# Sample unit of a chunked state-space scan: state transposes, bank pairs and copies in another order

## The chip, the cores and the metric

One core of a Trainium2 chip runs the whole step. The metric is the device time of one execution in microseconds, the median of the runs. Engines are named as in the profile: PE is TensorE (matmuls and transposes), DVE is VectorE, ACT is ScalarE, POOL is GpSimd, SP is the queue that issues the DMAs (SPq in a row).

## What is computed

One step of a decoder layer for 512 prompt tokens and 64 sample tokens (8 sequences of 8). The change lies in one stage of it, the scan of branch A. Cut to what matters:

```
# per group g (4) and head h (8 of 64 columns), 128 state columns; chunks of 128 prompt tokens, then the samples
y_diag = (cb * exp(seg) ) @ (dt * x)                  # within the chunk
y_off  = (c @ h_prev) * exp(a_cs)                     # from the state before the chunk
h_next = exp(a_cs[-1]) * h_prev + b^T @ (w_end * x)   # the state after it
y      = y_diag + y_off + d * x
y      = rms_norm(y * silu(u @ w_z)) * g              # the gate z is a product of its own
```

For the samples h_prev is not the running state but one state of 512 x 128 per sequence and group, read from memory, and every one of the 8 is written back renewed.

## The kernel before

The scan (stage_ssd) runs over 20 units k, five for each of the four groups g: four prompt chunks of 128 rows, then the sample unit with 64 rows, i = NT - 1 (k = 4, 9, 14, 19). Each engine has its own loop over k, written out by hand; within an engine the order is that of the code, and engines meet only in semaphores. In iteration k, PE does inputs(k) (transposes x and b, the product cb), gate(k - 1) (24 products for z into bank 7), turn(k - 2) (transposes the finished y) and outputs(k - 1). DVE does the front part of unit k (up to eight subtractions at L2040) and the back part of unit k - 1 (L2066 to L2099). ACT copies, and takes silu, exp and sqrt, with a table load between two of these kinds.

The sample unit's outputs are the long part. Its names:

- own heads: 8 small products of the unit itself (L1779), which need w_out (weigh, L2017) and scaled (POOL's xdt, xend, xd, L1708).
- last state: the running state is transposed into bank 6 (L1790); ACT copies it out (last_state, L1924).
- turn_states(j), j = 0 to 3 (a round): 8 transposes of two old states h0 (L1807) into two banks, bank 2 and 3 for even j, 6 and 7 for odd j. ACT copies the first bank (old_state, L1932), DVE the second (L2060), into h0T, which holds two rounds.
- POOL multiplies the two states of the round in place by their decay once they have been transposed (aging, L1724, two instructions a round, eight in all, counted in aged).
- old_part(j): 2 products (L1814) of round j; after the last one y_ready lets DVE's L2066 start, whose end raises y_step.
- new_part(q), q = 0 to 3: products (L1835) for the renewed states, each two banks of a 128-row quarter; DVE adds them to h0 (renew, L2010, two instructions a quarter, counted in hs_out). new_part(1) waits for L2066, new_part(2) and (3) wait for the first two renews.
- z_high and z_low (L1907, L1994): ACT and DVE split the next group's gate weights in two halves of 128x2048 each, u = 2g + 2 and 2g + 3. Both halves use the same raw buffer; the load of the second (SP, L1651) is issued when z_low of the first is done. In the last group merge_high and merge_low (L1946, L2000, 128x1024) stand there instead.
- decay(k) is ACT's exp of the next unit (L1892), weigh(k) DVE's product that needs it (L2017).

With k = 4, the first sample unit, the numbers are: gate(4), old rounds 0 to 3 of group 0, z halves 2 and 3, decay(5) and weigh(5) of the next unit, gate(5).

Of the kernel before, what the change touches and what calls it, by code (L numbers as in the profile page):

```python
# [13 lines left out]
ACT = mybir.ActivationFunctionType  # L14
AX = mybir.AxisListType.X

P = 128
# [5 lines left out]
NT = 5  # L23
ROWS = [P, P, P, P, NS]
# [39 lines left out]
K_ID = 0  # L64
# [1531 lines left out]
def stage_ssd(nc, io, sb):  # L1596

    with ExitStack() as ctx:
# [29 lines left out]
        NEW_BANK = (2, 5, 5, 2)  # L1628
        FIRST_BANK = (1, 7)
# [16 lines left out]
        with nc.Block() as block:  # L1646
# [81 lines left out]
            def _(pe):  # L1728
# [41 lines left out]
                def outputs(k):  # L1770
                    g, i = unit(k)
                    n = ROWS[i]
                    at = slice(P * i, P * i + n)
# [6 lines left out]
                    if i < NT - 1:  # L1780
                        pe.wait_ge(st_new, NT * g + i + 1)
                        if g >= 1 and i == 0:
                            pe.wait_ge(hs_out, 8 * g - 2)
                        pe.matmul(banks[0:n, 5, :], sb.xbcT[:, 20 + g, at], stT[:], start=True, stop=True).then_inc(y_ready, 1)
                        pe.matmul(banks[0:NST, 6, :], b_t[0:n, k % 2, :], xend[0:n, k % 2, :], start=True, stop=True).then_inc(st_ready, 1)
                        return

                    pe.wait_ge(st_new, NT * (g + 1))
# [3 lines left out]
                    pe.wait_ge(h_in, 64 * (g + 1))  # L1792
                    pe.wait_ge(of_seq, g + 1)

                    def turn_states(j):

                        if j == 0 and g >= 1:
                            pe.wait_ge(hs_out, 8 * g)
                        elif j == 1:
                            pe.wait_ge(fin_out, g + 1)  # L1800
                            pe.wait_ge(z_out, k + 1)
                        elif j >= 2:
                            pe.wait_ge(hT_out, 4 * g + j - 1)
                            pe.wait_ge(hT_out2, 4 * g + j - 1)
                        for a, b in enumerate((j, j + 4)):
                            for q in range(4):
                                mm = pe.transpose(banks[:, (2, 6)[j % 2] + a, q * P:(q + 1) * P], h0[:, q, b, :], K[:, K_ID:K_ID + P])  # L1807
                        mm.then_inc(hT_ready, 1)
# [7 lines left out]

                    turn_states(0)
                    turn_states(1)
                    old_part(0)
                    old_part(1)  # L1820
# [41 lines left out]
                for k in range(N + 2):  # L1862
                    late = k >= 2 and unit(k - 2)[1] == NT - 1
                    if k < N:
                        inputs(k)
                    if late:
                        new_part(k - 2, 1)
                    if k == N + 1:
                        first_merge()
                    if 1 <= k <= N:  # L1870
                        gate(k - 1)
                    if late:
                        new_part(k - 2, 2)
                        new_part(k - 2, 3)
                    if k >= 2:
                        turn(k - 2)
                    if 1 <= k <= N:
                        outputs(k - 1)

            @block.scalar  # L1880
            def _(act):
# [44 lines left out]
                def old_state(g, m):  # L1926
                    act.wait_ge(hT_ready, 4 * g + m + 1)
                    if m >= 2:
                        act.wait_ge(off_part, 3 * g + m - 1)
                    elif g >= 1:  # L1930
                        act.wait_ge(y_ready, NT * g)
                    act.activation(h0T[:, 2 * (m % 2), :], banks[:, (2, 6)[m % 2], :], ACT.Copy).then_inc(hT_out, 1)  # L1932
# [16 lines left out]
                for k in range(N + 2):  # L1949
# [3 lines left out]
                    if sample_now:  # L1953
                        g = unit(k - 1)[0]
                        gate_out(k - 1)
                        if g + 1 < G:
                            z_high(2 * g + 2)
                        else:
                            merge_high(0)
                        turned_y(k - 2)  # L1960
                        last_state(g)
                        old_state(g, 0)
                        old_state(g, 1)
                        if k < N:
                            decay(k)
                        old_state(g, 2)
                        old_state(g, 3)
# [20 lines left out]
            def _(dve):  # L1988
# [30 lines left out]
                for k in range(N + 1):  # L2019
# [24 lines left out]
                    if k >= 1:  # L2044
# [4 lines left out]
                        if i == NT - 1:  # L2049
                            if g + 1 < G:  # L2050
                                z_low(2 * g + 2)
                            else:
                                merge_low(0)
                            for m in range(4):
                                dve.wait_ge(hT_ready, 4 * g + m + 1)
# [4 lines left out]
                                dve.tensor_copy(h0T[:, 2 * (m % 2) + 1, :], banks[:, (3, 7)[m % 2], :]).then_inc(hT_out2, 1)  # L2060
                                if m == 1 and k < N:
                                    weigh(k)
# [1112 lines left out]
```

## Time and profile before

| what | us |
|---|---|
| median of three runs | 2369.98 |
| the three runs | 2366.33 to 2376.86 |
| the profiled execution's own time | 2370.28 |
| its span | 2368.5 |
| PE busy, share of the span | 2267.1 (96%) |
| DVE busy | 1839.4 (78%) |
| ACT busy | 1339.6 (57%) |
| POOL busy | 493.4 (21%) |

The profile is of one execution. The scan lies between 654 and 926 us from the span's start; the four sample units begin near 703, 769, 834 and 899 us, the expert stage fills the second half of the span. A timeline row gives start, duration, engine, line, instruction, output and input, shapes, a count where equal rows are merged, and in brackets the idle time before it and what ended it. For POOL a duration includes time in which the instruction was started but could not run. Matmul rows overlap, since the array is pipelined: the distance between starts is what one costs.

### The profile page before, as it was taken

What the parts mean: (1) busy time and instruction counts of PE and PEld (TensorE: products, weight loads), DVE (VectorE), ACT (ScalarE), POOL (GpSimd) and SP (SyncE); (2) the same over time, 40 slices, a digit from 0 to 9 for tenths busy, and PEclk for the clock granted to TensorE, in tenths of its full rate; (3) what the DMA queues carried; (4) which work ended last, traced back from release to release, by engine and by line L of the source; (5) the groups of instructions that cost most, each with busy time, mean ns of one, the idle gap of its engine ahead of it and who ended that gap; (6) DMA issues with size and microseconds to landing.
All of it is one profiled execution on the core that took longest, in us unless ns stands there. A gap on an engine that the chain in (4) does not pass through costs nothing. (4 is left out here: it accounts for less than half of the span.)

```text
span 2368.5 us, 36101 instructions
## 1 busy us (share of the span) xinstructions
PE 2267.1 (96%) x13249; PEld 1839.9 (78%) x13249; DVE 1839.4 (78%) x2245; ACT 1339.6 (57%) x1462; POOL 493.4 (21%) x414
## 2 busy tenths in 40 slices
PE   8898999999999999998789999999999999999997
PEld 5484558999876667997677888888888888888884
DVE  2577764268788886345679999999999999999997
ACT  1352224133366775213257777777777777777774
POOL 0202410000035452002081221221221221221223
PEclk9998999999989999999799999999999999999999
DMA  5307864242134444327199999999999999999994
GB/s 178 148 1 247 295 244 111 55 154 86 42 115 147 143 123 134 123 74 230 63 308 401 394 396 395 381 382 392 381 381 395 380 381 394 382 376 395 383 378 184
DMA packets 253187, 602.38 MB, mean 254 GB/s; under 512 B 31136, under 2 KB 122657, under 8 KB 248092
## 3 DMA queue, kind: packets, MB, share of 16 engines
q1 hardware_dynamic: 235396, 522.98, 60.3%
q0 software_dynamic: 17680, 77.88, 10.3%
q8 instruction: 74, 1.21, 0.2%
q14 instruction: 37, 0.30, 0.0%
HBM read 558.20 MB, written 42.61 MB: 254 GB/s over the span
## 5 line engine op out<-in xcount | busy, mean ns | idle before, releaser
L2931 DVE TENSOR_TENSOR w_lo<-w_raw,w_hi 128x2048 fp32r<-128x2048 f32 x291 | 658.6, 2288 | 50.0 <-ACT w_hi L2876 47.6
L2876 ACT ACTIVATE w_hi<-w_raw 128x2048 fp32r<-128x2048 f32 x288 | 550.2, 1916 | 112.1 <-PE banks L2786 90.0
L2786 PE MATMUL banks<-w_hi,x_hi 128*128 128x512 f32 x1024 | 319.6, 393 | 4.7 <-DVEq L2976 3.4
L2786 PE MATMUL banks<-w_lo,x_hi 128*128 128x512 f32 x1024 | 316.5, 390 | 0.0
L2786 PE MATMUL banks<-w_hi,x_lo 128*128 128x512 f32 x1024 | 315.8, 390 | 0.0
L2931 DVE TENSOR_TENSOR w_lo<-mergedT,w_hi 128x2048 fp32r<-128x2048 f32 x96 | 220.0, 2292 | 34.3 <-ACT w_hi L2876 33.7
L2786 PEld LDWEIGHTS banks<-w_lo,x_hi 128*128 128x128 f32 x1024 | 192.6, 188 | 40.8
L2786 PEld LDWEIGHTS banks<-w_hi,x_lo 128*128 128x128 f32 x1024 | 192.5, 188 | 40.9
L2786 PEld LDWEIGHTS banks<-w_hi,x_hi 128*128 128x128 f32 x1024 | 190.2, 188 | 43.0 <-DVEq L2976 3.7
L2734 POOL DMA_INDIRECT y_sum<-xT,to_row x31 | 51.0, 1645 | 817.8 <-ACT xT L2913 777.9
L2876 ACT ACTIVATE w_hi<-mergedT 128x2048 fp32r<-128x2048 f32 x96 | 183.8, 1915 | 34.5 <-PE banks L2786 30.7
L2786 PE MATMUL banks<-w_hi,h_hi 128*128 128x512 f32 x512 | 161.5, 397 | 0.0
L2786 PE MATMUL banks<-w_lo,h_hi 128*128 128x512 f32 x512 | 158.5, 391 | 0.0
L2786 PE MATMUL banks<-w_hi,h_lo 128*128 128x512 f32 x512 | 157.8, 389 | 0.0
L2786 PEld LDWEIGHTS banks<-w_lo,h_hi 128*128 128x128 f32 x512 | 96.4, 188 | 20.7
L2786 PEld LDWEIGHTS banks<-w_hi,h_lo 128*128 128x128 f32 x512 | 96.1, 188 | 20.8
L2786 PEld LDWEIGHTS banks<-w_hi,h_hi 128*128 128x128 f32 x512 | 93.9, 189 | 17.8 <-DVE h_lo L2935 0.3
L1253 DVE TENSOR_TENSOR ws_lo<-room,ws_hi 128x1024 fp32r<-128x1024 f32 x22 | 27.0, 1226 | 82.4 <-ACT ws_hi L1231 82.4
L1426 PE MATMUL banks<-xs_hi,ws_hi 128*128 128x288 f32 x384 | 84.2, 301 | 3.9 <-DVE ws_lo L1500 3.9
L2885 ACT ACTIVATE xT<-banks 128x512 f32<-128x512 f32 x64 | 38.5, 601 | 82.4 <-PE banks L2792 82.4
L1426 PE MATMUL banks<-xs_hi,ws_lo 128*128 128x288 f32 x384 | 83.2, 298 | 0.0
L1426 PE MATMUL banks<-xs_lo,ws_hi 128*128 128x288 f32 x384 | 83.2, 298 | 0.0
(542 smaller groups left out, 4614.6 us busy)
## 6 DMA issues: line engine op xcount, KB each, us to landing
w_raw<-in_exp_w_gu SPq DMA_DIRECT2D x196, 1024.0 KB, 10.0
w_raw<-in_exp_w_down SPq DMA_DIRECT2D x96, 1024.0 KB, 7.0
mergedT<-in_exp_w_gu SPq DMA_DIRECT2D x64, 1024.0 KB, 9.1
mergedT<-in_exp_w_down SPq DMA_DIRECT2D x32, 1024.0 KB, 9.8
w_x<-in_w_in SPq DMA_DIRECT2D x11, 1024.0 KB, 5.4
xT<-in_w_in SPq DMA_DIRECT2D x9, 1024.0 KB, 7.5
room<-acs_rows SPq DMA_DIRECT2D x16, 512.0 KB, 4.0
mergedT<-in_state_ssm SPq DMA_DIRECT2D x16, 512.0 KB, 6.8
```

The source lines that it names most:

```text
L1253: dve.tensor_tensor(w_lo[:, u % NW], w_raw[u % NR], w_hi[:, u % NW].bitcast(F32), ALU.subtract).then_inc(w_low, 1)
L1426: mm = pe.matmul(banks[:, b + piece, 0:H2], wp[:, c % 2, k, at:at + P], part[:, k, piece * H2:(piece + 1) * H2], start=(k == 0 and wp is w ...
L2734: pool.indirect_dma_start(out=io.y_sum, out_offset=bass.IndirectOffsetOnAxis(ap=to_row[:, par, :].bitcast(U32), axis=0), in_=y_out, in_off ...
L2786: mm = pe.matmul(banks[:, bank + c, :], x[:, k, :], part[:, s % NHI, j, c * 512:(c + 1) * 512], start=start, stop=last)
L2876: act.activation(w_hi[:, s % NHI], raw(s, par), ACT.Copy).then_inc(hi_ready, 1)
L2885: act.activation(halves(sg), pair(h)[:, :, :, 0], ACT.Sigmoid, scale=SW_ALPHA).then_inc(sig_out, 1)
L2931: dve.tensor_tensor(w_lo[:, s % NHI], raw(s, par), w_hi[:, s % NHI].bitcast(F32), ALU.subtract).then_inc(lo_ready, 1)
```

## The change

PE, sample unit: round 0 is transposed ahead of gate(k - 1); the last state's transposes come directly behind the gate; old_part(0), round 1, the own heads, round 2, old_part(1), round 3, old_part(2), new_part(0), old_part(3) follow the turn of y. Rounds 0 and 1 now use banks 2 and 3, rounds 2 and 3 banks 6 and 7 (OLD_BANK), so that round 1 waits for the copies of round 0, round 2 for the last state's and the gate's readers, round 3 for the copies of round 2. ACT takes the copy of round 0 ahead of silu, the last state's copy behind it, and the exp of the next unit behind all four copies. DVE takes copies 0 and 1 ahead of z_low, and weigh of the next unit behind copy 3. The number of instructions is the same. new_part, old_part and the two helper bodies themselves are unchanged.

```diff
+        OLD_BANK = (2, 2, 6, 6)
-                def outputs(k):
+                def own_part(k):
...
+                def turn_states(k, j):
+                    g = unit(k)[0]
+                    if j == 0:
+                        pe.wait_ge(h_in, 64 * (g + 1))
+                        if g >= 1:
+                            pe.wait_ge(hs_out, 8 * g)
+                    elif j == 2:
+                        pe.wait_ge(fin_out, g + 1)
+                        pe.wait_ge(z_out, k + 1)
+                    else:
+                        pe.wait_ge(hT_out, 4 * g + j)
+                        pe.wait_ge(hT_out2, 4 * g + j)
+                    for a, b in enumerate((j, j + 4)):
+                        for q in range(4):
+                            mm = pe.transpose(banks[:, OLD_BANK[j] + a, q * P:(q + 1) * P], h0[:, q, b, :], K[:, K_ID:K_ID + P])
+                    mm.then_inc(hT_ready, 1)
...
-                    turn_states(0)
-                    turn_states(1)
+                    pe.wait_ge(of_seq, g + 1)
+                    pe.wait_ge(y_step, 2 * k - 1)
                     old_part(0)
+                    turn_states(k, 1)
+                    own_part(k)
+                    turn_states(k, 2)
                     old_part(1)
-                    turn_states(2)
-                    turn_states(3)
+                    turn_states(k, 3)
                     old_part(2)
+                    new_part(k, 0)
                     old_part(3)
-                    new_part(k, 0)
...
+                    sample_now = 1 <= k <= N and unit(k - 1)[1] == NT - 1
+                    if sample_now:
+                        turn_states(k - 1, 0)
                     if 1 <= k <= N:
                         gate(k - 1)
+                    if sample_now:
+                        last_state(k - 1)
...
-                    if 1 <= k <= N:
+                    if sample_now:
+                        sample_outputs(k - 1)
+                    elif 1 <= k <= N:
                         outputs(k - 1)
```

ACT around the first sample unit. Before (table load and silu at L1900, z_high at L1907, last state at L1924, rounds at L1932, exp at L1892):

```order
378 L1900 ACT_TABLE_LOAD
379 L1900 ACTIVATE zs<-banks 64x512
380 L1907 ACTIVATE ws_hi<-xT 128x2048
381 L1917 ACTIVATE xbcT<-banks,gnT 128x128 x4
382 L1924 ACTIVATE mergedT<-banks 128x512
383 L1932 ACTIVATE xT<-banks 128x512 x2
384 L1892 ACT_TABLE_LOAD
385 L1892 ACTIVATE room<-room 128x1024
386 L1932 ACTIVATE xT<-banks 128x512 x2
387 L1907 ACTIVATE ws_hi<-xT 128x2048
```

ACT after the change (the same bodies at L1917, L1924, L1941, L1949 and L1909):

```order
378 L1949 ACTIVATE xT<-banks 128x512
379 L1917 ACT_TABLE_LOAD
380 L1917 ACTIVATE zs<-banks 64x512
381 L1941 ACTIVATE mergedT<-banks 128x512
382 L1924 ACTIVATE ws_hi<-xT 128x2048
383 L1949 ACTIVATE xT<-banks 128x512
384 L1934 ACTIVATE xbcT<-banks,gnT 128x128 x4
385 L1949 ACTIVATE xT<-banks 128x512 x2
386 L1909 ACT_TABLE_LOAD
387 L1909 ACTIVATE room<-room 128x1024
388 L1924 ACTIVATE ws_hi<-xT 128x2048
```

The exp and its table load moved from between rounds 1 and 2 to behind round 3, still ahead of the second z_high.

DVE at the same place, before (L1994 z_low, L2060 rounds, L2017 weigh of the next unit):

```order
778 L2040 TENSOR_SCALAR room<-room,acs 128x128 x8
779 L1994 TENSOR_TENSOR ws_lo<-xT,ws_hi 128x2048
780 L2060 COPY xT<-banks 128x512 x2
781 L2017 TENSOR_TENSOR room<-room,aend 128x1024
782 L2060 COPY xT<-banks 128x512 x2
783 L2066 TENSOR_TENSOR y<-banks,e_acs 64x512
784 L1994 TENSOR_TENSOR ws_lo<-xT,ws_hi 128x2048
785 L2074 TENSOR_TENSOR y<-y,xd 64x512
```

DVE after the change (L2011 z_low, L2077 rounds, L2034 weigh, L2083 the first step of y):

```order
778 L2057 TENSOR_SCALAR room<-room,acs 128x128 x8
779 L2077 COPY xT<-banks 128x512 x2
780 L2011 TENSOR_TENSOR ws_lo<-xT,ws_hi 128x2048
781 L2077 COPY xT<-banks 128x512 x2
782 L2034 TENSOR_TENSOR room<-room,aend 128x1024
783 L2083 TENSOR_TENSOR y<-banks,e_acs 64x512
784 L2011 TENSOR_TENSOR ws_lo<-xT,ws_hi 128x2048
785 L2091 TENSOR_TENSOR y<-y,xd 64x512
```

z_low moved behind the copies of rounds 0 and 1, and weigh from between the rounds to directly ahead of the first step of y.

## Rows read from the trace of the kernel before

**Rows 1.** Windows: start:end, length, busy us (x count) per engine, clock, DMA.

```profile
711.00:725.00 14.00, 11.35 (x68) 6.19 (x66) 9.75 (x9) 8.49 (x13) 12.75 (x8) 1.00 0.41 121
731.00:765.00 34.00, 34.00 (x198) 26.02 (x194) 33.10 (x71) 25.62 (x43) 12.36 (x12) 1.00 0.61 182
903.00:916.00 13.00, 12.77 (x87) 7.33 (x85) 6.07 (x10) 7.86 (x15) 8.21 (x8) 1.00 0.03 11
926.00:935.00 9.00, 6.67 (x30) 6.70 (x31) 3.01 (x5) 3.62 (x7) 0.00 (x0) 0.62 0.86 233
```

**Rows 2.** Timeline of PE, first sample unit, gate(4) to new_part(2).

```profile
703.38 0.48 PE L1767 MATMUL banks<-ws_hi,xs_hi 128*64 128x512 f32 x1
...
708.97 0.60 PE L1847 MATMUL banks<-const,y 128*128 128x128 f32 x4
...
711.07 1.04 PE L1807 MATMUL banks<-const,mergedT 128*128 128x128 f32 x8
713.11 1.09 PE L1807 MATMUL banks<-const,mergedT 128*128 128x128 f32 x8 [1.01 <-ACT mergedT L1924]
714.64 1.91 PE L1814 MATMUL banks<-xT,t 128*32 128x512 f32 x8 [0.43 <-DVE xT L2060]
...
719.65 1.91 PE L1814 MATMUL banks<-xT,t 128*32 128x512 f32 x8 [1.20 <-DVE xT L2060]
721.49 1.13 PE L1835 MATMUL banks<-b_of,xend 32*128 32x512 f32 x4
...
730.31 1.99 PE L1835 MATMUL banks<-b_of,xend 32*128 32x512 f32 x8
```

**Rows 3.** Timeline of DVE over the same unit.

```profile
704.21 0.69 DVE L2079 TENSOR_TENSOR y<-y,zs 128x512 f32<-128x512 f32 x1
...
708.20 1.65 DVE L2040 TENSOR_SCALAR room<-room,acs 128x128 f32<-128x128 f32 x8
711.60 2.29 DVE L1994 TENSOR_TENSOR ws_lo<-xT,ws_hi 128x2048 fp32r<-128x2048 f32 x1 [1.75 <-ACT ws_hi L1907]
713.80 1.28 DVE L2060 COPY xT<-banks 128x512 f32<-128x512 f32 x2
717.24 1.66 DVE L2017 TENSOR_TENSOR room<-room,aend 128x1024 f32<-128x1024 f32 x1 [2.15 <-ACT room L1892]
...
721.60 0.68 DVE L2066 TENSOR_TENSOR y<-banks,e_acs 64x512 f32<-64x512 f32 x1 [1.50 <-PE banks L1814]
722.20 2.27 DVE L1994 TENSOR_TENSOR ws_lo<-xT,ws_hi 128x2048 fp32r<-128x2048 f32 x1
724.40 1.53 DVE L2074 TENSOR_TENSOR y<-y,xd 64x512 f32<-64x512 f32 x1
...
727.85 2.40 DVE L2010 TENSOR_TENSOR mergedT<-mergedT,banks 128x512 f32<-128x512 f32 x4
```

**Rows 4.** Timeline of ACT, from the exp of the next unit on.

```profile
714.85 1.28 ACT L1892 ACT_TABLE_LOAD   x1
716.15 1.06 ACT L1892 ACTIVATE room<-room 128x1024 f32<-128x1024 f32 x1
...
718.98 1.91 ACT L1907 ACTIVATE ws_hi<-xT 128x2048 fp32r<-128x2048 f32 x1
```

**Rows 5.** Timeline of POOL: the first, the second and the last aging instruction.

```profile
712.25 2.55 POOL L1724 TENSOR_TENSOR mergedT<-mergedT,t 128x512 f32<-128x512 f32 x1 [10.73 <-PE banks L1807]
...
714.76 1.05 POOL L1724 TENSOR_TENSOR mergedT<-mergedT,t 128x512 f32<-128x512 f32 x1
...
721.78 3.61 POOL L1724 TENSOR_TENSOR mergedT<-mergedT,t 128x512 f32<-128x512 f32 x1
```

**Rows 6.** Timeline of DVE in the next unit: weigh (L2017) while POOL is idle.

```profile
740.82 1.22 DVE L2017 TENSOR_TENSOR room<-room,aend 128x1024 f32<-128x1024 f32 x1
```

**Rows 7.** Line L1651 (gate weights): the load issued at 713.9, then all six.

```profile
DMA to landing us min/median/max: 5.0/5.0/5.0
...
DMA to landing us min/median/max: 5.0/6.6/9.8
```

More of the change, by code:

```diff
@@ L1768, in gate @@
                     mm.then_inc(z_ready, 1)
-                def outputs(k):
-                    g, i = unit(k)
-                    n = ROWS[i]
-                    at = slice(P * i, P * i + n)
+                def own_part(k):
+                    n = ROWS[unit(k)[1]]
                     pe.wait_ge(w_out, k + 1)
@@ L1779, in outputs, with last_state @@
                         pe.matmul(banks[0:n, 4, h * PD:(h + 1) * PD], dec[0:n, k % 3, h, 0:n], xdt[0:n, k % 2, h * PD:(h + 1) * PD], start=True, stop=True)
[L1780 to L1788, printed above, removed]
+                def outputs(k):
+                    g, i = unit(k)
+                    n = ROWS[i]
+                    at = slice(P * i, P * i + n)
+                    own_part(k)
+                    pe.wait_ge(st_new, NT * g + i + 1)
+                    if g >= 1 and i == 0:
+                        pe.wait_ge(hs_out, 8 * g - 2)
+                    pe.matmul(banks[0:n, 5, :], sb.xbcT[:, 20 + g, at], stT[:], start=True, stop=True).then_inc(y_ready, 1)
+                    pe.matmul(banks[0:NST, 6, :], b_t[0:n, k % 2, :], xend[0:n, k % 2, :], start=True, stop=True).then_inc(st_ready, 1)
+                def turn_states(k, j):
[14 more added lines that the diff above has]
+                    mm.then_inc(hT_ready, 1)
+                def last_state(k):
+                    pe.wait_ge(st_new, NT * (unit(k)[0] + 1))
                     for q in range(4):
@@ L1791, in outputs, with sample_outputs @@
                     mm.then_inc(fin_ready, 1)
[L1792 to L1808, printed above, removed]
+                def sample_outputs(k):
+                    g = unit(k)[0]
                     def old_part(j):
@@ L1931, in old_state @@
                         act.wait_ge(y_ready, NT * g)
-                    act.activation(h0T[:, 2 * (m % 2), :], banks[:, (2, 6)[m % 2], :], ACT.Copy).then_inc(hT_out, 1)
+                    act.activation(h0T[:, 2 * (m % 2), :], banks[:, OLD_BANK[m], :], ACT.Copy).then_inc(hT_out, 1)
                 def root(j):
@@ L1954, in _ @@
                         g = unit(k - 1)[0]
+                        old_state(g, 0)
                         gate_out(k - 1)
+                        last_state(g)
                         if g + 1 < G:
@@ L1959, in _ @@
                             merge_high(0)
+                        old_state(g, 1)
                         turned_y(k - 2)
[L1961 to L1963 removed]
+                        old_state(g, 2)
+                        old_state(g, 3)
                         if k < N:
                             decay(k)
[L1966 to L1967 removed]
                         if g + 1 < G:
@@ L2049, in _ @@
                         if i == NT - 1:
[L2050 to L2053, printed above, removed]
                             for m in range(4):
+                                if m == 2 and g + 1 < G:
+                                    z_low(2 * g + 2)
+                                elif m == 2:
+                                    merge_low(0)
                                 dve.wait_ge(hT_ready, 4 * g + m + 1)
@@ L2059, in _ @@
                                     dve.wait_ge(y_ready, NT * g)
-                                dve.tensor_copy(h0T[:, 2 * (m % 2) + 1, :], banks[:, (3, 7)[m % 2], :]).then_inc(hT_out2, 1)
-                                if m == 1 and k < N:
-                                    weigh(k)
+                                dve.tensor_copy(h0T[:, 2 * (m % 2) + 1, :], banks[:, OLD_BANK[m] + 1, :]).then_inc(hT_out2, 1)
+                            if k < N:
+                                weigh(k)
                         dve.wait_ge(y_ready, j + 1)
```

1 line of the change is left out of this document (added).

## The prediction

> **What bounds the kernel now.** The table of busy times comes first: PE is busy for 96% of the span, so only PE's holes and what it waits for can give time back. The windows view then shows where the scan has holes. In the first sample unit PE works 11.35 us of 14.00, so 2.65 us are idle; between two sample units it works 34.00 of 34.00; in the last sample unit 12.77 of 13.00 [rows 1]. The first three sample units read alike, shifted by about 65 us each. So the change plays in three windows with 2.65 us of holes each and one with 0.23: 8.2 us in all, 0.35% of the time. PE's timeline names the holes: 1.01 us before round 1, 0.43 before the old parts, 1.20 before the last two old parts, the last two for DVE's copies [rows 2]. Since PE has no hole between sample units, whatever a sample unit loses is carried on to the next one and to the end.
>
> Then DVE. After y_ready it runs nearly without a pause: L2066 at 721.60, z_low at 722.20, L2074 at 724.40, the renews from 727.85 to 730.25 [rows 3], and new_part(2) starts at 730.31 [rows 2]. Gate(5) ends there as well: it starts at about 724.5 and takes 5.6 us (703.38 to 708.97 for gate(4)). So at this point PE and DVE are level, and a DVE chain that is later by x makes PE wait x. That is the wait that will end last.
>
> POOL and DVE block each other. An aging instruction takes 1.05 us, but the first one took 2.55 and ended at 714.80, 0.91 after DVE's z_low (711.60 + 2.29 = 713.89); the last took 3.61 and ended at 725.39, 0.92 after z_low at 724.47 [rows 3, 5]. In return L2074, started at 724.40, took 1.53 and ended at 725.93, 0.54 after POOL's. Weigh took 1.66 during aging [rows 3] and 1.22 with POOL idle [rows 6]. L2066, which reads a matmul bank, took 0.68 in the middle of aging. So a DVE instruction with both inputs in SBUF and a POOL instruction exclude each other for their whole length, and each waits for the one that is running. The Trainium skill says this too (SBUF — State Buffer, "SBUF: two separate sides"): the port pair of the two engines is an exclusive lock, and whoever starts first has it for the whole instruction. It speaks against a change that spreads aging over more of DVE's work; the last rival below says what the time would be without it.
>
> **The change part by part, first sample unit.** I place each step at its time in the trace. A round costs PE 0.9 and is readable 1.1 after its start (1.04 in the row), an old part 0.92 (half of 1.84), a new part 0.95, the last state 0.5, the turn of y 0.5, the own heads 1.07 (two rows' distance, 708.97 to 711.07, less these two), inputs about 0.9 [rows 2]; a copy of a bank 0.6 to 0.7 [rows 3].
>
> 1. Round 0 ahead of the gate: PE 703.35 to 704.25, gate to 709.85, last state and turn to 710.9. On PE this is moved work, no more.
> 2. POOL now starts aging at 704.5 instead of 712.25. There it meets L2079 and its followers [rows 3]. Two POOL instructions of 0.9 get in between them, of which DVE had about 0.3 spare: DVE is 0.65 later, its subtractions (708.20 + 1.65 = 709.85) end at 710.5, copy 0 at 711.2. old_part(0) starts at 711.35 rather than at 710.9. What was hidden work of POOL costs PE 0.45 here.
> 3. old_part(0), round 1 (readable 713.4), own heads, round 2 (readable 715.4), old_part(1), to 716.1. The 1.01 us hole before round 1 is filled, since own heads stand between.
> 4. DVE has copy 1 from 713.4 to 714.1, then z_low. POOL's third aging instruction holds the lock until 714.4, so z_low ends at 716.6 (2.2 us of work) and copy 2 at 717.25. Round 3 needs copy 2: 717.4 to 718.3, readable 718.5. The hole that was ahead of the last old parts is now ahead of round 3, 1.3 us against 1.20.
> 5. Copies 3 end at 719.15. old_part(2), new_part(0), old_part(3) run from 718.3 to 721.1: y_ready at 721.2 instead of 721.56. The own reordering of PE gives 0.35 here, and 1.4 more to inputs, as new_part(0) is done already.
> 6. ACT's exp now comes behind copy 3: 719.15 + 1.28 table load + 1.06 [rows 4] = 721.5. Weigh on DVE, which stood at 717.24 in a hole, takes 1.22 from there: 722.7, and L2066 behind it ends at 723.35 instead of 722.28. **This is where the sign turns:** +1.05 on DVE's chain although y_ready is earlier. If POOL's next instruction gets the lock first, weigh ends 1.0 later still.
> 7. The second z half: its load is issued when z_low is done, 716.6 instead of 713.89, and lands 5.0 us later [rows 7], 721.6. ACT takes 1.91 [rows 4]: 723.55. z_low then finds POOL inside an instruction until 724.6 and ends at 726.8, against 724.47: +2.3.
> 8. From there to the second renew it was 5.78 us before (724.47 to 730.25), with one POOL instruction in the way, and POOL, which has xd(5) left, is in the way again: renews end at 732.45. PE: inputs from 721.1, new_part(1) after L2066 at 723.5, gate(5) 724.55 to 730.15, then 2.3 us of waiting, new_part(2) at 732.5 instead of 730.31. **+2.2 us.** Had POOL won in step 6, gate(5) would end at 731.2 and the renews at 732.6, +2.3.
>
> Bounds of it: with no lock waits in steps 6 to 8 and z_low at 723.6, it ends at 725.8, L2074 at 726.4 and the renews at 730.75: +0.45. With one more POOL instruction in the way (1.05) it is +3.3. I take +2.2, since POOL has eleven instructions in a row (eight of aging, three of the next unit) and is thus always busy there.
>
> SP: the weights' load is the one DMA that moves (+2.7 us). The loads of old states are issued behind the renews and have four units' time until round 0 needs them.
>
> The last sample unit has no next unit: no exp, no weigh, 128x1024 splits. Aging two instructions earlier delays DVE as in step 2, and silu's table load comes behind copy 0. From the same steps y_ready moves from 914.6 to 915.2: +0.6 (bounds -0.2, its idle time in rows 1, and +1.5).
>
> Sum: 3 x 2.2 + 0.6 = **+7.2 us**, on 2370.28 of the profiled execution 2377.5. That execution stands 0.3 above the median, so I say **2377**. With the bounds: +1.2 to +11.4, 2371 to 2381.
>
> **The rivals.**
>
> - *The holes are filled and DVE keeps up.* PE's chain alone: old_part(3) ends at 721.1, inputs 722.0, new_part(1) and gate(5) 1.5 us earlier than before. 3 x 1.5 = 4.5 gives 2366; all holes of rows 1 would be 8.2 and give 2362. It needs L2066 done by 722 and the renews by 728.8, so exp done before 720 and no lock waits behind it. For it: 2.65 us of holes are there. Against: exp is behind copy 3, and DVE had no slack at 730.25. Chance 0.14.
> - *The weights come late into gate(5).* Its second half needs the second z half at 724.55 + 2.8 = 727.35, and the forecast has it at 726.8. From a landing time of 5.6 us on, PE waits within the gate and everything behind it follows. The three loads in this place landed in 5.0 to 5.2, the slowest of the line in 9.8 [rows 7]. At 8 us a sample unit costs 2.2 + 2.5 or so, in three 14, and 2385. Chance 0.07.
> - *The clock falls in the longer wait.* After PE's pause at the end of the stage the granted clock was 0.62 over 9 us [rows 1], so 1.2 GHz for some 6.8 of them. If the 2.3 us before new_part(2) did the same three times, up to 3.4 us each would be added: 2387. Against: the holes of 1.0 and 1.2 us leave it at 1.00 [rows 1], and PE is busy on both sides. Chance 0.05.
> - *No lock waits in the moved places.* If aging and z_low fall apart by luck, the lower bound holds: 3 x 0.45 + 0.6 = +2, 2372. Chance 0.20. By the Trainium skill's rule (SBUF — State Buffer, "SBUF: two separate sides"), a lock for the whole instruction, this does not happen; by shared bandwidth it would.
>
> **How the numbers follow.** The forecast has 0.54. Rival one is faster than before, but by 0.2 to 0.35%, and the runs before spread over 10.5 us. A difference under 0.5% (11.85 us) is about what a measurement of this kernel can tell from no change. Faster by more needs more than all holes: 0.02. Slower by more needs 2381.8: rivals two and three and the forecast's upper tail, 0.15. Within: 0.83. The range from 2364 to 2386 leaves out the deepest part of rival one and the upper parts of two and three; it has 3 us of the runs' own scatter at either end of the bounds.
>
> **What the changed profile would show.** POOL's first aging instruction at about 704.5, and DVE's subtractions 0.65 later. A PE hole of over 1 us before round 3 instead of before round 1. Weigh directly ahead of L2066, and L2066 released by weigh and not by PE; ACT's exp at 720.4. The second z_low near 724 and long. The renews released by nothing but DVE itself, and a PE wait of about 2 us before new_part(2), which is the mark of the forecast; if it is not there and gate(5) starts before 724, rival one is right. A hole within gate(5) marks rival two, matmuls of doubled length behind new_part(2) rival three. The time from gate(4)'s start to new_part(2), 27.0 us before, should read 29.2 from round 0's start. I would be wrong above all if POOL's and DVE's turns at the lock come in another order than I replayed, since eleven and seven instructions meet there.

## The result

The changed kernel takes 2390.17 us (median of six runs, 2388.59 to 2394.73) against 2372.22 for the kernel before on the same chips (2365.77 to 2376.86). The ratio is 1.0081, 95% interval 1.0069 to 1.0093: 18 us slower by the medians and 19 by the ratio, clear of noise and above the stated range of 2364 to 2386. Five of the kernels below ran once; of these the timelines are read, and the total says little. The profiled execution has a span of 2390.7 us, 22.2 more than before.

The stage tells where it went. From PE's first to the next stage's first instruction the scan took 274.2 us before and 290.9 after, +16.7. The stretch ahead of the scan is 1.2 us longer in this one profile and the one behind it 4.3; I come back to the latter. Within the scan:

| piece of the scan | before | after | difference |
|---|---|---|---|
| start to the first sample unit | 49.2 | 47.9 | -1.3 |
| sample units 1 to 3, start to new_part(2), each | 26.93 | 28.95 | 3 x 2.02 |
| new_part(2) to the next sample unit | 38.46, 38.46, 37.37 | 41.67, 43.23, 40.94 | +3.2, +4.8, +3.6 |
| last sample unit, start to new_part(2) | 24.54 | 24.98 | +0.4 |

So 6.5 us come from the sample units and 11.5 from the stretches between them, which the change does not touch. The first row is no gain of the change: in the profile of the kernel before, the granted clock stood at 0.50 for 17.1 us around the start of the scan, in that of the changed kernel for 13.7, and late_age below, with 17.1 again, has 49.3 us there. Like for like the scan became 18 us longer.

### PE at the first sample unit, after

The timeline of PE (start, duration, engine, line, ..., count, idle before and what ended it), to set against [rows 2]:

```profile
703.29 1.04 PE L1806 MATMUL banks<-const,mergedT 128*128 128x128 f32 x8
...
710.95 1.05 PE L1822 MATMUL banks<-xT,t 128*32 128x512 f32 x4 [0.24 <-DVE xT L2077]
...
717.05 1.06 PE L1806 MATMUL banks<-const,mergedT 128*128 128x128 f32 x8 [0.95 <-DVE xT L2077]
...
723.02 1.13 PE L1845 MATMUL banks<-b_of,xend 32*128 32x512 f32 x4 [0.97 <-DVE y L2083]
732.24 1.99 PE L1845 MATMUL banks<-b_of,xend 32*128 32x512 f32 x8 [2.30 <-DVE mergedT L2027]
734.15 0.46 PE L1857 MATMUL banks<-const,y 64*128 64x64 f32 x4
734.54 3.66 PE L1778 MATMUL banks<-xdt,room 128*128 128x64 f32 x16
```

The reader is to see two things. The last wait of the sample unit, 2.30 us for DVE's renews, is new. And the own heads behind it, the same 16 products in the same place of the order, take 3.66 us; in the kernel before they took 2.00:

```profile
732.62 2.00 PE L1779 MATMUL banks<-xdt,room 128*128 128x64 f32 x16
```

### DVE and ACT, after

DVE over the same stretch, to set against [rows 3]:

```profile
708.55 1.65 DVE L2057 TENSOR_SCALAR room<-room,acs 128x128 f32<-128x128 f32 x8
...
713.67 2.63 DVE L2011 TENSOR_TENSOR ws_lo<-xT,ws_hi 128x2048 fp32r<-128x2048 f32 x1
716.23 0.68 DVE L2077 COPY xT<-banks 128x512 f32<-128x512 f32 x1
...
721.15 1.23 DVE L2034 TENSOR_TENSOR room<-room,aend 128x1024 f32<-128x1024 f32 x1 [2.31 <-ACT room L1909]
722.29 0.68 DVE L2083 TENSOR_TENSOR y<-banks,e_acs 64x512 f32<-64x512 f32 x1
723.82 2.61 DVE L2011 TENSOR_TENSOR ws_lo<-xT,ws_hi 128x2048 fp32r<-128x2048 f32 x1 [0.85 <-ACT ws_hi L1924]
726.35 1.53 DVE L2091 TENSOR_TENSOR y<-y,xd 64x512 f32<-64x512 f32 x1
...
729.78 2.41 DVE L2027 TENSOR_TENSOR mergedT<-mergedT,banks 128x512 f32<-128x512 f32 x4
```

ACT's exp and second split high half, to set against [rows 4]:

```profile
720.06 1.06 ACT L1909 ACTIVATE room<-room 128x1024 f32<-128x1024 f32 x1
721.88 1.91 ACT L1924 ACTIVATE ws_hi<-xT 128x2048 fp32r<-128x2048 f32 x1 [0.76 <-DMA xT<-in_w_in]
```

The chain reads: first split done at 716.3, load landed at 721.9, high half to 723.8, low half to 726.4 (0.35 us of it waiting for POOL), L2091 held by POOL until 727.3, renews done at 732.2.

### The clock

Windows view (start:end, length, then busy us and count for PE, PEld, DVE, ACT and POOL, granted clock, DMA share, GB/s). Behind the three new_part(2), after:

```profile
734.60:741.40 6.80, 6.80 (x21) 4.74 (x21) 5.39 (x15) 3.43 (x7) 2.82 (x3) 0.50 0.71 202
741.40:772.00 30.60, 30.60 (x180) 24.65 (x179) 28.52 (x58) 22.46 (x38) 11.25 (x11) 1.00 0.48 141
802.90:813.10 10.20, 10.20 (x31) 6.21 (x32) 6.71 (x17) 5.83 (x10) 3.04 (x3) 0.50 0.69 201
878.00:884.80 6.80, 6.80 (x21) 4.63 (x21) 5.84 (x16) 2.82 (x5) 2.20 (x3) 0.50 0.66 187
```

and at the like places of the kernel before:

```profile
733.00:739.80 6.80, 6.80 (x39) 5.27 (x39) 6.70 (x17) 3.36 (x7) 2.49 (x3) 1.00 0.64 186
798.00:804.80 6.80, 6.80 (x40) 5.35 (x39) 6.70 (x17) 3.50 (x7) 2.88 (x3) 1.00 0.68 203
864.00:870.80 6.80, 6.80 (x38) 5.21 (x38) 6.70 (x17) 3.36 (x6) 2.27 (x3) 1.00 0.67 194
```

PE gets 21 matmuls done in a window where it did 39 before, and the granted clock is 0.50 (1.2 GHz) instead of 1.00 (2.4 GHz). Nearly all of the 11.5 us of the table goes with 23.8 us at the lower level; the kernel fill below, with the clock at 1.00, has stretches of 38.54, 38.53 and 37.77, so the clock's part is 3.1, 4.7 and 3.2, together 11.0, and 0.4 us of the third difference is something else. The busy share of PE, 6.80 of 6.80 in both, tells nothing of it.

### The profile page after: what moved, and what is told of

Same layout as the page of the kernel before. It is cut to its first block and busy times, and to the rows that moved or that the text cites. A ratio compares the mean times of both kernels' runs of the same rounds, so it can differ in the third digit from the quotient of the medians.

```text
span 2390.7 us, 36104 instructions
## 1 busy us (share of the span) xinstructions
PE 2286.0 (96%) x13249; PEld 1854.0 (78%) x13249; DVE 1845.9 (77%) x2245; ACT 1340.0 (56%) x1462; POOL 492.4 (21%) x414
## 3 DMA queue, kind: packets, MB, share of 16 engines
q0 software_dynamic: 17680, 77.88, 10.2%
## 5 line engine op out<-in xcount | busy, mean ns | idle before, releaser
L1709 POOL TENSOR_TENSOR xdt<-xs_t,dt 128x512 f32<-128x512 f32 (+1 forms) x20 | 27.8, 1391 | 293.3 <-ACT xs_t L1904 270.4
```

Source lines behind the costliest of these rows:

```text
L1709: ins = pool.tensor_tensor(heads(o[0:n, k % 2], n), x, f[:, g * HG:(g + 1) * HG].unsqueeze(2).broadcast_to((n, HG, PD)), ALU.mult)
```

## Experiments

Two questions stood open. Does the granted clock fall because of the 2.30 us wait (theory W), or because of the reordered transposes and short products ahead of it (theory T)? And why are the renews 2 us later: exp and weigh ahead of L2083 (E, the prediction's step 6), or the second weight split (Z, its step 7), and how much of it is the lock? In the table "sample" is the time from the first instruction of round 0 (or of the gate, in the old order) to new_part(2), and "scan" runs from PE's first instruction of the stage to the first of the next, both taken from PE's timeline.

| kernel | sample, units 1 to 3 | wait before new_part(2) | low clock behind it | scan | time, us (before on the same chip) |
|---|---|---|---|---|---|
| before | 26.93 | 0 | 0 of 3 | 274.2 | 2372.2 |
| changed | 28.95 | 2.30 | 3 of 3 | 290.9 | 2390.2 |
| fill | 28.93 | 0.09 | 0 of 3 | 279.9 | 2379.15 (2368.98) |
| before_hole | 29.38 | 2.38 | 3 of 3 | 291.1 | 2385.63 (2368.98) |
| before_half_hole | 28.19 | 1.20 | 1 of 3 | 279.7 | 2377.26, one run (2371.46) |
| own_first | 28.94, 28.93, 28.29 | 0.58, 0.57, 0 | 1 of 3 | 279.1 | 2377.90 (2368.98) |
| noage | 26.70, 26.66, 26.52 | 0.4 to 0.6 | 0 of 3 | 272.9 | 2368.89, one run (2368.98) |
| exp_mid | 28.88 | 2.70 | 3 of 3 | 292.0 | 2386.91, one run (2369.28) |
| late_age | 28.63, 28.63, 27.69 | 2.30, 2.30, 1.32 | 3 of 3 | 291.8 | 2385.96, one run (2369.28) |
| old_copies | 34.26, 34.17, 33.62 | 1.01, 1.00, 1.00 | 2 of 3 | 309.0 | 2406.33, one run (2369.28) |
| split_early | 26.78 | 2.16 | 3 of 3 | 284.4 | 2380.99 (2369.28) |
| best_fill | 26.08 | 0 | 0 of 3 | 271.3 | 2369.67 (2371.46) |
| best_own | 26.27 | 0 | 0 of 3 | 271.8 | 2371.72 (2371.46) |
| best_fill4 | 24.97 | 0 | 0 of 3 | 268.1 | 2372.94 (2369.69) |

### Is it the wait? fill and before_hole

```diff
                    # fill, PE, changed kernel
+                    if late and k <= N:
+                        for f in range(20):
+                            pe.matmul(banks[:, 1, 320:512], sb.x_hi[:, f % 8, 0:P], z_half(sb.ws_hi, 0)[:, f % 4, 0:192], start=True, stop=True)
                     if late:
                         new_part(k - 2, 2)
```

> The changed kernel with 20 extra products of 128x192 on PE (into a part of bank 1 that nobody reads) between gate(5) and new_part(2), where PE waits 2.30 us; the same at the second and third sample unit. Theory W (the granted clock falls because of this wait): no stretch at 0.5 inside the scan, sample unit still 28.9 to 29.2 us from round 0 to new_part(2), but the 11.5 us between the sample units go; scan from 290.9 to about 279 us, total about 2378 to 2380. Theory T (it falls because of the reordered transposes and short products ahead of gate(5)): three stretches at 0.5 remain, scan stays at about 290, total about 2390.

Measured: 2379.15 us (ratio 1.0044, 1.0027 to 1.0061). Each taken against the kernel before on its own chip, that is 8 us less than the changed kernel by the medians and 9 by the ratios, although PE has 60 matmuls more. The sample unit is as long as before (28.93), only the wait is filled:

```profile
730.82 2.37 PE L1889 MATMUL banks<-ws_hi,xs_hi 128*128 128x192 f32 x20
733.28 1.99 PE L1845 MATMUL banks<-b_of,xend 32*128 32x512 f32 x8
```

and the windows behind it have the clock at 1.00 in all three places:

```profile
735.60:742.40 6.80, 6.80 (x40) 5.36 (x39) 6.70 (x17) 3.48 (x7) 2.86 (x3) 1.00 0.69 202
803.00:809.80 6.80, 6.80 (x41) 5.29 (x39) 6.70 (x17) 3.55 (x7) 2.93 (x3) 1.00 0.70 205
```

Everything that T blames is still there. T falls, and the clock's price is read off the two profiles: 290.9 - 279.9 = 11.0 us of scan.

The counterpart puts the wait into the old order:

```diff
                    # before_hole, DVE, kernel before
+                            if g + 1 < G:
+                                for a in range(2):
+                                    dve.memset(h0T[:, 1::2, :], 0.0).then_inc(paused, 1)
+                                    dve.wait_ge(paused, 2 * g + a + 1)
                             dve.wait_ge(aged, 4 * (g + 1))
                             renew(j, 0)
```

> The kernel before, in its old order, with a pause of two memsets (about 2.1 us in all) on DVE ahead of the renews in the first three sample units, so that PE waits about 2 us before new_part(2). Theory W: stretches at 0.5 behind new_part(2) in most of the three places, scan from 274.2 to about 290 (3 x 2.1 of wait and 3 x 3 to 5 of low clock), total about 2385 to 2390. Theory T: clock stays at 1.00, scan about 280.5, total about 2376.

Measured: 2385.63 us (ratio 1.0070, 1.0054 to 1.0087), scan 291.1. PE's row at the first place and the windows behind two of the three:

```profile
732.74 1.99 PE L1836 MATMUL banks<-b_of,xend 32*128 32x512 f32 x8 [2.38 <-DVE mergedT L2011]
```

```profile
806.50:813.30 6.80, 6.80 (x22) 4.63 (x21) 5.77 (x16) 2.94 (x5) 2.33 (x3) 0.50 0.68 191
874.80:881.60 6.80, 6.80 (x25) 4.16 (x26) 5.18 (x11) 4.63 (x9) 3.04 (x3) 0.50 0.82 249
```

A wait of 2.4 us and nothing else of the change gives nearly the whole loss of the changed kernel. W holds both ways, for a wait in this place.

### How long a wait? before_half_hole

```diff
                    # before_half_hole, DVE: one memset instead of two
-                                for a in range(2):
-                                    dve.memset(h0T[:, 1::2, :], 0.0).then_inc(paused, 1)
-                                    dve.wait_ge(paused, 2 * g + a + 1)
+                                dve.memset(h0T[:, 1::2, :], 0.0).then_inc(paused, 1)
+                                dve.wait_ge(paused, g + 1)
```

> The kernel before with one memset (about 1.05 us) as the pause on DVE instead of two, so a wait of about 1.3 us before new_part(2). Waits of 2.2 us and more were followed by a low clock every time (12 of 12), waits of 0.6 us and less once in nine, those of 1.0 to 1.3 three times in four. Theory W then expects one to three stretches here, scan 280 to 289, total 2374 to 2384. None would say that the length of the wait is not what matters.

Measured: wait 1.20 us in all three places, low clock behind one of them. Counted over all kernels, for waits before new_part(2) alone (the expectation's 12 of 12 should have read 14 of 14): waits of 2.15 us and more were followed by a low clock in 14 of 14 places, waits of 1.00 to 1.32 in 4 of 7, of 0.4 to 0.6 in 1 of 5, of 0.1 and less in none of 16. The same wait of 1.20 us was followed by it once and not twice in one execution, so the length alone does not decide below 2.

The place matters too. PE's waits of 1.01 and 1.20 us ahead of round 1 and the last old parts [rows 2] were followed by no low clock in any of the three sample units of the kernel before, nor were five waits of 1.45 to 1.48 us in the stretches between sample units (own_first, best_own) and two of 1.98 us ahead of round 3 (old_copies), of which this is one:

```profile
799.92 1.07 PE L1806 MATMUL banks<-const,mergedT 128*128 128x128 f32 x8 [1.98 <-DVE xT L2077]
```

The pause of 2.95 us at the stage's end had a stretch of 0.50 with it in all fourteen profiles. What in the work around new_part(2) makes a wait there count for more than one ahead of a round, no run here varies.

### What makes the renews late? exp_mid, late_age, noage

```diff
                    # exp_mid, ACT, changed kernel
-                        old_state(g, 3)
                         if k < N:
                             decay(k)
+                        old_state(g, 3)
```

> The changed kernel with one of its moves undone on ACT: the next unit's exp stands between the copies of round 2 and round 3 (718.1 instead of 721.1 for its end), weigh stays where it is on DVE. Theory Z (the renews are late because the second weight split is: its load, issued when the first split is done, lands at 721.9): L2083 and new_part(1) come 1.0 us earlier, but the second split still starts at 723.8, new_part(2) stays at 28.9 us from round 0, and PE's wait before it grows from 2.3 to about 3.3 us. Theory E (the step of the prediction where the sign turns, exp and weigh ahead of L2083, makes the renews late): new_part(2) comes 1.0 us earlier, 27.9.

Measured: new_part(1) comes 1.0 us earlier (18.7 instead of 19.7 us after the start of the unit), new_part(2) at 28.88 as in the changed kernel. The wait there is 2.70, not the 3.3 expected: another part of PE's lead is spent inside gate(5), in a wait of 0.33 us for the split. The rows of ACT and PE:

```profile
716.22 0.60 ACT L1949 ACTIVATE xT<-banks 128x512 f32<-128x512 f32 x1
719.45 1.91 ACT L1924 ACTIVATE ws_hi<-xT 128x2048 fp32r<-128x2048 f32 x1 [2.63 <-DMA xT<-in_w_in]
```

```profile
724.49 0.51 PE L1768 MATMUL banks<-ws_hi,xs_hi 128*128 128x512 f32 x1 [0.33 <-DVE ws_lo L2011]
730.24 1.99 PE L1845 MATMUL banks<-b_of,xend 32*128 32x512 f32 x8 [2.70 <-DVE mergedT L2027]
```

Z stands and E falls: with exp out of the way ACT merely waits 2.63 us for the load, where it waited 0.76 in the changed kernel.

```diff
                    # late_age, POOL, changed kernel
+                        pool.wait_ge(fin_ready, g + 1)
                         for j in range(4):
                             pool.wait_ge(hT_ready, 4 * g + j + 1)
```

> The changed kernel with POOL's first aging held back until the last state is transposed (710.3 instead of 704.5), so that it no longer meets DVE's back part of the chunk before. Step 2 of the prediction says this lock costs DVE 0.65 us (measured 0.4) and old_part(0) 0.24: copy 0 ends 0.4 us earlier, old_part(0) has no wait, new_part(2) at 28.7 instead of 28.95. If the early aging helps anything, it gets longer.

Measured: 28.63 instead of 28.95, copy 0 on DVE half a us earlier from the unit's start, no wait before old_part(0). The lock cost of step 2 is real and small. In the third sample unit it was 27.69. There DVE's second split got ahead of a POOL instruction that it had waited for in the first:

```profile
724.09 3.15 DVE L2012 TENSOR_TENSOR ws_lo<-xT,ws_hi 128x2048 fp32r<-128x2048 f32 x1 [0.31 <-ACT ws_hi L1925]
867.72 2.29 DVE L2012 TENSOR_TENSOR ws_lo<-xT,ws_hi 128x2048 fp32r<-128x2048 f32 x1 [0.17 <-ACT ws_hi L1925]
```

One turn at the lock was worth 0.9 us; the third unit of own_first (28.29) shows the same pattern, 2.29 us for the split against 2.88.

The third leaves out POOL's aging altogether; its old states are written back undecayed:

```diff
                    # noage, POOL, changed kernel
-                            for b in (j, j + 4):
-                                ins = pool.tensor_tensor(h0[:, :, b, :], h0[:, :, b, :], e_seq[:, :, b:b + 1].broadcast_to((P, 4, NST)), ALU.mult)
-                            ins.then_inc(aged, 1)
+                            pool.sem_inc(aged, 1)
```

> The changed kernel with POOL's aging left out (the old states are not decayed, semaphores raised all the same), so that nothing contends with DVE in the sample unit but the three products for the next unit. Prediction's bound without lock waits: sample unit 27.4 us from round 0 to new_part(2) instead of 28.95, old_part(0) 0.2 us earlier. If the lock is not what makes DVE late, it stays at 28.9.

Measured: 26.70, 0.7 below the bound that I had given and 0.2 below the kernel before:

```profile
722.42 2.29 DVE L2009 TENSOR_TENSOR ws_lo<-xT,ws_hi 128x2048 fp32r<-128x2048 f32 x1 [0.30 <-ACT ws_hi L1922]
724.62 0.68 DVE L2089 TENSOR_TENSOR y<-y,xd 64x512 f32<-64x512 f32 x1
...
727.20 2.40 DVE L2025 TENSOR_TENSOR mergedT<-mergedT,banks 128x512 f32<-128x512 f32 x4
```

L2089 takes 0.68 us where it took 1.53, the split 2.29 where it took 2.61. So without aging, and with it most waits at the lock, the first sample unit of the changed kernel is 2.25 us shorter, about as much as it had become longer (2.02). Waits at the lock exist in the kernel before as well; how much they cost there was not measured. That DVE could lose some of them in its hole of 2.15 us [rows 3] is my reading.

### Is it the order of PE or that of the copies? old_copies

```diff
                    # old_copies: PE and banks as changed, ACT (and likewise DVE) as before
-                        old_state(g, 0)
                         gate_out(k - 1)
-                        last_state(g)
                         if g + 1 < G:
                             z_high(2 * g + 2)
...
-                        old_state(g, 1)
                         turned_y(k - 2)
-                        old_state(g, 2)
-                        old_state(g, 3)
+                        last_state(g)
+                        old_state(g, 0)
+                        old_state(g, 1)
                         if k < N:
                             decay(k)
+                        old_state(g, 2)
+                        old_state(g, 3)
```

> PE's new order and new bank pairs alone: ACT and DVE have the order of the kernel before (split first, exp and weigh between round 1 and 2). old_part(0) then waits for copy 0 behind the split on both engines, until about 714.6 instead of 710.95, so new_part(0) comes 1.5 to 3 us later; the second split starts earlier than in the changed kernel. If the copies' order is what costs the 2.0 us, new_part(2) comes at 27 or below; if it is PE's order, at 29.5 to 31.

Measured: 34.2, outside both forecasts. PE waits 4.62 us for copy 0 and then does the rounds with the granted clock at 0.50:

```profile
717.83 1.92 PE L1822 MATMUL banks<-xT,t 128*32 128x512 f32 x4 [4.62 <-DVE xT L2077]
719.68 1.97 PE L1806 MATMUL banks<-const,mergedT 128*128 128x128 f32 x8
721.58 1.97 PE L1778 MATMUL banks<-xdt,room 64*64 64x64 f32 x16
```

PE's new order needs the early copies. The other half, the new order of the copies under PE's old order, was not run, so the 2.0 us are not divided between the two.

### Real work in the wait: own_first

```diff
                    # own_first, PE, changed kernel; outputs(k) then leaves its own_part out
+                    if late and k <= N:
+                        own_part(k - 1)
                     if late:
                         new_part(k - 2, 2)
```

> The changed kernel with the next unit's own heads (1.9 us of PE) moved from behind new_part(2), new_part(3) and the turn of y to between gate(5) and new_part(2). Own heads need L2093 of the sample unit (ends 728.6), so they fit in the wait (729.9 to 732.2). Theory W: wait of 0.3 to 0.5 us left, no stretch at 0.5, and 1.9 us less of work behind new_part(2): scan 290.9 - 11.5 - 3 x 1.9 = about 274, as in the kernel before, total about 2370. Theory T: scan about 285, total 2384. If the round is then bound by DVE behind the renews, up to 3 x 1.5 of it is not gained.

Measured: 2377.90 us (ratio 1.0041, 1.0027 to 1.0055), scan 279.1, hardly better than fill with its useless products, though 1.9 us of work left the stretch behind new_part(2). The last clause of the expectation is what happened, and in full: from new_part(2) to the next sample unit it is 38.54 and 38.52 us here, 38.54 and 38.53 in fill. The first of these holds although 3.4 us of it ran with the clock at 0.50. Where the clock stayed at 1.00, PE now stands still in that stretch until DVE has a y ready:

```profile
809.73 0.66 PE L1858 MATMUL banks<-const,y 128*128 128x128 f32 x4 [1.45 <-DVE y L2119]
```

So DVE has no slack there either. PE's 34.00 busy of 34.00 [rows 1] does not show it, but DVE's 33.10 of 34.00 in the same row does.

### A shorter chain: split_early, and the best versions

```diff
                    # split_early, ACT, changed kernel (DVE: the first z_low ahead of copy 1)
                         old_state(g, 0)
-                        gate_out(k - 1)
-                        last_state(g)
+                        act.activation(warm[:], K[0:1, 0:1], ACT.Silu)
                         if g + 1 < G:
                             z_high(2 * g + 2)
...
+                        gate_out(k - 1)
+                        last_state(g)
                         old_state(g, 1)
                         turned_y(k - 2)
                         old_state(g, 2)
-                        old_state(g, 3)
                         if k < N:
                             decay(k)
+                        old_state(g, 3)
```

> The changed kernel with the first split moved forward: ACT makes its high half directly behind the gate (its silu table is loaded early by a silu of one element), DVE its low half ahead of copy 1, while POOL is idle and DVE was too; exp between round 2 and 3. Theory Z: the load is issued 2.2 us earlier (714.1), lands at 719.1, the second split starts at about 721.0 and new_part(2) is at 26.1 to 26.6 us from round 0, below the 26.9 of the kernel before. PE's wait before it is 1.5 to 2 us, so by theory W the clock may still fall in some places; scan 271 with the clock at 1.00, up to 280 with three falls.

Measured: 2380.99 us (ratio 1.0043, 1.0026 to 1.0060). The load lands at 719.2, the second split starts 2.65 us earlier than in the changed kernel, and the sample unit falls to 26.78, just under the kernel before. Yet it is 11.7 us slower than that, since PE's wait is still there:

```profile
719.23 1.91 ACT L1925 ACTIVATE ws_hi<-xT 128x2048 fp32r<-128x2048 f32 x1 [0.77 <-DMA xT<-in_w_in]
```

```profile
729.92 2.75 PE L1846 MATMUL banks<-b_of,xend 32*128 32x512 f32 x8 [2.16 <-DVE mergedT L2029]
```

The expectation had the sample unit at 26.1 to 26.6, the wait at 1.5 to 2 us and the scan at 280 at most. The clock's part is plain here: a sample unit that is as short as before, in a scan that is 10.2 us longer.

```diff
                    # best_fill and best_own, DVE, on top of split_early
+                        dve.wait_ge(y_step, 2 * j + 1)
+                        dve.wait_ge(scaled, j + 1)
+                        dve.tensor_tensor(y[0:n, j % 2, :], y[0:n, j % 2, :], xd[0:n, j % 2, :], ALU.add).then_inc(y_sum, 1)
                         if i == NT - 1 and g + 1 < G:
                             z_low(2 * g + 3)
                         elif i == NT - 1:
                             merge_low(1)
-                        dve.wait_ge(y_step, 2 * j + 1)
-                        dve.wait_ge(scaled, j + 1)
-                        dve.tensor_tensor(y[0:n, j % 2, :], y[0:n, j % 2, :], xd[0:n, j % 2, :], ALU.add).then_inc(y_sum, 1)
```

> split_early with two more edits: on DVE the addition L2091 stands ahead of the second weight split (it fills a hole of 0.4 us there and takes a lock wait off the chain), and 14 extra products of 128x192 on PE fill its wait before new_part(2). Theory W and Z together: new_part(2) 25.5 to 26.5 us from round 0, no stretch at 0.5 inside the scan, scan 270 to 273 us (before: 274.2, with a quieter start of the stage than this), total 2365 to 2369. If W were wrong the three stretches stay and the total is 2376 to 2381.

> As best_fill, but with the next unit's own heads (real work, 1.9 us) in the place of the extra products. Wait before new_part(2) of 0 to 0.5 us. In own_first one of three such short waits was followed by a low clock, so 0 to 1 stretch here: scan 270 to 275, total 2365 to 2371. The stretch between the sample units was 38.5 us with own heads in either place, so their move itself saves nothing.

Measured: best_fill 2369.67 us (ratio 0.9996, 0.9987 to 1.0005), best_own 2371.72 (1.0003, 0.9992 to 1.0013). Sample unit 26.08 and 26.27, no wait, clock at 1.00, scan 271.3 and 271.8. Both repair the loss; neither is measurably faster than the kernel before, and both totals lie a little above what was expected. The scan is 2.4 to 2.8 us shorter than before, and 1.3 us of that are the start of the stage, as in the first table.

best_fill4 is best_fill with `range(4)` in the place of `range(14)`:

> best_fill with 4 extra products instead of 14: there the second renew ended 1.2 us before PE was through with the extra products (728.9 against 730.1), so they had become the bound. With 4 (0.46 us) new_part(2) should come 24.9 to 25.1 us from round 0 instead of 26.1, with at most 0.1 us of wait and the clock at 1.00; scan 3 x 1.1 shorter, 268 to 269 us, total 3 us under best_fill: 2365 to 2368. If the stretch behind is bound by DVE in a way that does not follow, the sample unit is shorter and the scan is not.

```profile
730.49 0.58 PE L1890 MATMUL banks<-ws_hi,xs_hi 128*128 128x192 f32 x4
731.00 1.99 PE L1846 MATMUL banks<-b_of,xend 32*128 32x512 f32 x8
```

Measured: the sample unit is at 24.97 and the scan at 268.1, 6.1 us under the kernel before, as expected, but the whole is 2372.94 us (ratio 1.0014, 1.0006 to 1.0023) instead of 2365 to 2368, no gain at all. In its profile all but the scan takes 11 us more than in that of the kernel before: 3.8 of them ahead of the scan, and the rest in a wait of 10.0 us near the end of PE's work, which is 2.7 us in the kernel before and 2.65 to 3 in best_fill and best_own. Whether that wait is a matter of this one execution or belongs to the kernel, one profile can't tell. Where the scan's gain goes in the median stays open.

## Why the prediction was wrong

**Right, step by step.** The replay of the sample unit gave 29.2 us from round 0 to new_part(2); it measured 28.95. POOL's first aging stood at 704.48 (forecast 704.5):

```profile
704.48 2.62 POOL L1725 TENSOR_TENSOR mergedT<-mergedT,t 128x512 f32<-128x512 f32 x2 [3.14 <-PE banks L1806]
713.11 8.13 POOL L1725 TENSOR_TENSOR mergedT<-mergedT,t 128x512 f32<-128x512 f32 x6 [6.01 <-PE banks L1806]
```

The hole before round 3 was 0.95 us (forecast 1.3), L2083 ended at 722.97 (723.35), the second split ended at 726.43 (726.8), the renews at 732.19 (732.45), and PE's wait was 2.30 (2.3). The last sample unit lost 0.4 (0.6). The sum of these terms, 7.2 in the forecast, measured 3 x 2.02 + 0.4 = 6.5.

**The step that failed** is the sum: 3 x 2.2 + 0.6 has the new wait of 2.3 us before new_part(2) and nothing for the clock behind it. The clock was put aside as the third rival, "the clock falls in the longer wait", with a chance of 0.05, and what that rival said would happen did: PE at the lower level behind new_part(2) in all three places, 11.0 us of scan by fill. Its price, up to 3.4 us each, was near too (3.1, 4.7 and 3.2). The argument against it failed: that the holes of 1.0 and 1.2 us had left the clock at 1.00, and that PE was busy on both sides. A hole of 1.2 us says nothing on one of 2.3, and the trace had a case nearer to it, the pause of 2.95 us at the stage's end with the clock at 0.62 behind it [rows 1]. The forecast made a new wait of 2.3 us in the middle of TensorE's work and then asked only what it costs while it lasts. 6.5 + 11.5 = 18 us is what the changed scan costs when both are counted, the difference of the medians. With the rival in the sum at its own price the forecast would have been 2387, above the stated range too.

**Right sign, wrong culprit.** Step 6 marked exp and weigh ahead of L2083 as the place where the sign turns. exp_mid shows that they are covered: it is step 7, the load that can only be issued when the first split is done, that sets the renews, and step 6 cost nothing of its own. The sum did not suffer, since it took the renews from step 7.

**The lock.** The lower bound, "no lock waits, +0.45", was for steps 6 to 8; with aging gone from the whole unit it measured -0.23 (noage). The Trainium skill's rule (SBUF — State Buffer, "SBUF: two separate sides"), an exclusive lock for a whole instruction, agrees: the addition of xd to y took 1.53 us with POOL at work (L2091, changed kernel) and 0.68 without (L2089, noage). The rival that put 0.20 on the absence of such waits did not come: L2091 and the second split (2.61 us against 2.29) both waited.

**The weights coming late into gate(5)** did not happen in the changed kernel: the load landed 5.5 us after its issue, below the 5.6 named. It happens, with a wait of 0.33 us, once PE arrives earlier (exp_mid).

**"Whatever a sample unit loses is carried on to the end"** held, but the reason given is half of it. PE has next to no slack between the sample units: 6.8 us at the lower level, up to 3.4 us of lost work, made the stretch 3.1 us longer. DVE has none either: 1.9 us less work on PE made it no shorter (own_first). The two are level, so a gain on PE alone gives nothing there.

**The rest.** Of the 22.2 us between the two spans 4.3 lie behind the scan: 3.5 in the first experts, where the granted clock stood at 0.50 for 10.2 us instead of 3.4, and 1.3 near the end, where it stood there for 6.8 instead of 3.4; 0.5 were gained between. The medians differ by 18 us, so this part need not belong to the change; no run here settles it.

## What to carry to other kernels

When a change creates or lengthens a wait of TensorE in the midst of its work, price it twice: the wait, and the matmuls behind it at half the clock. Here each sample unit became 2.0 us longer, with 2.3 us of waiting in it, and the stretch behind it 3.1 to 4.7 more, and it paid to fill the wait, even with products that nobody reads. A low clock is also worth looking for wherever two profiles differ outside the change. When steps are moved ahead of a transfer's trigger, follow the trigger: the buffer shared by two loads, not the reordered arithmetic, set the new end.

## What was not expected of the hardware

A wait of 2.15 us and more before new_part(2) was followed by a granted clock of 0.50 for 6.8 to 10.2 us every time (14 places); at 1.20 us the same kernel showed both outcomes in one execution, and even one wait of 0.58 us was followed by 3.4 us of low clock:

```profile
732.20:735.60 3.40, 3.17 (x5) 1.41 (x5) 3.40 (x10) 2.41 (x6) 2.86 (x3) 0.50 0.95 279
```

PE's busy share hardly tells: it is 6.80 of 6.80 in the changed kernel's stretches and 3.17 of 3.40 here. Counting matmuls in equal windows (21 against 39), or reading the clock's column, is what shows it.
